# A later row turn, a re-ordered norm chain, four more taps on TensorE, and the last S5 weight loads behind the last state product

## Time and profile before

| what | us |
|---|---|
| median of 3 runs | 996.05 (995.78 to 996.17) |
| the profiled execution, its own time | 997.24 |
| its span, from first to last instruction | 995.4 |
| PE busy | 966.9 (97%) |
| DVE busy | 586.6 (59%) |
| ACT busy | 505.2 (51%) |
| POOL busy | 308.5 (31%) |
| mean granted TensorE clock | 0.993 of full speed |

### The profile page before, as it was taken

The page is one execution under the profiler, slowest core; times in us unless marked ns, Lnnn a source line. Parts: engine busy times, 40 slices in busy tenths (PEclk is TensorE's granted clock), DMA queues, the critical chain, the costliest instruction groups (busy, mean ns, idle before and its releaser), DMA issues.

```text
span 995.4 us, 14273 instructions
## 1 busy us (share of the span) xinstructions
PE 966.9 (97%) x5438; PEld 803.5 (81%) x5438; DVE 586.6 (59%) x643; ACT 505.2 (51%) x719; POOL 308.5 (31%) x331
## 2 busy tenths in 40 slices
PE   8999989999999989999999999999988999999997
PEld 6987768888878878888888888888978888888886
DVE  4899865555544455565674545446685764544534
ACT  5865455444443366446664444435465664444332
POOL 5770337888689505763010000000000020000000
PEclk9999899999999999999999999999999999999999
DMA  9832026676767727554446657567963455657541
GB/s 336 272 128 84 1 85 206 222 222 222 264 219 234 229 80 260 169 169 152 145 137 200 192 174 242 182 203 253 387 228 102 154 166 177 201 173 253 170 169 42
DMA packets 133827, 186.79 MB, mean 188 GB/s; under 512 B 5904, under 2 KB 104720, under 8 KB 133264
## 3 DMA queue, kind: packets, MB, share of 16 engines
q1 hardware_dynamic: 109632, 158.28, 49.1%
q10 hardware_dynamic: 24144, 27.81, 8.1%
HBM read 174.54 MB, written 15.73 MB: 191 GB/s over the span
## 4 chain that ended last, share of the span: by engine, by line
PE 85%; DVE 7%; DMA 3%; ACT 2%; issue 2%; POOL 1%; POOLq 0%; ACTq 0%; DVEq 0%
PE ps L508 24%; PE ps L480 15%; PE ps L482 14%; PE ps L481 14%; DVE cacc L2354 2%; PE ps L460 2%; PE ps L462 2%; PE ps L461 2%; DMA wraw<-in_w_in 2%; PE ps L1052 1%; PE ps L837 1%; PE ps L1071 1%; DMA O_dram<-ob 1%; PE ps L619 1%; PE ps L1157 1%
## 5 line engine op out<-in xcount | busy, mean ns | idle before, releaser
L420 DVE TENSOR_TENSOR wlo<-wraw,whi 128x2048 fp32r<-128x2048 f32 x127 | 303.1, 2388 | 298.2 <-ACT whi L414 298.2
L414 ACT ACTIVATE whi<-wraw 128x2048 fp32r<-128x2048 f32 x127 | 243.1, 1915 | 259.0 <-PE ps L482 159.5
L480 PE MATMUL ps<-whi,actH 128*128 128x512 f32 x640 | 257.8, 403 | 1.0 <-ACT qa L2107 0.6
L482 PE MATMUL ps<-whi,actL 128*128 128x512 f32 x640 | 250.2, 391 | 0.0
L481 PE MATMUL ps<-wlo,actH 128*128 128x512 f32 x640 | 249.4, 390 | 0.0
L480 PEld LDWEIGHTS ps<-whi,actH 128*128 128x128 f32 x640 | 120.3, 188 | 27.4 <-issue 2.3
L482 PEld LDWEIGHTS ps<-whi,actL 128*128 128x128 f32 x640 | 120.1, 188 | 26.1
L481 PEld LDWEIGHTS ps<-wlo,actH 128*128 128x128 f32 x640 | 120.5, 188 | 22.4
L754 POOL TENSOR_SCALAR ss<-ss 128x1 f32<-128x1 f32 x8 | 1.8, 220 | 439.6 <-ACT sg L724 439.6
L508 PE MATMUL ps<-whi,gH 128*128 128x512 f32 x248 | 77.8, 393 | 0.0
L508 PE MATMUL ps<-wlo,gH 128*128 128x512 f32 x248 | 76.8, 390 | 0.0
(11 more groups left out here) (452 smaller groups left out, 1574.2 us busy)
## 6 DMA issues: line engine op xcount, KB each, us to landing
wraw<-in_ffn_w_gate SPq DMA_DIRECT2D x44, 512.0 KB, 4.0
wraw<-in_ffn_w_up SPq DMA_DIRECT2D x44, 512.0 KB, 5.0
wraw<-in_ffn_w_down SPq DMA_DIRECT2D x18, 1024.0 KB, 4.9
wraw<-in_fox_w_in SPq DMA_DIRECT2D x16, 1024.0 KB, 5.5
wraw<-in_w_gate SPq DMA_DIRECT2D x22, 512.0 KB, 4.0
wraw<-in_w_up SPq DMA_DIRECT2D x22, 512.0 KB, 5.0
wraw<-in_w_in SPq DMA_DIRECT2D x9, 1024.0 KB, 11.4
wraw<-in_w_down SPq DMA_DIRECT2D x9, 1024.0 KB, 5.5
```

The costliest lines, as they stand in the source:

```text
L414: act.activation(self.high_of(n0), self.wraw[:, n0 % RAW, :], ACT.Copy).then_inc(self.hi_done, 1)
L420: dve.tensor_tensor(self.low_of(n0), self.wraw[:, n0 % RAW, :], self.high_of(n0).bitcast(F32), ALU.subtract).then_inc(self.lo_done, 1)
L480: pe.matmul(out, xh, wh, start=(ka == 0), stop=False)
L482: last = pe.matmul(out, xl, wh, start=False, stop=(ka == KT - 1))
```

## The change

It does the following. (a) `turn(1, 1)` moves from (row 1, unit n) to (row 0, unit n+1), in `f1` and `fp`. In `fp` the forget logits move back by two quarters, and their turn goes behind the whole of unit n+2; ACT splits n+2 ahead of the two squares, DVE ahead of the copy of the logits. (b) `SHARED` goes from 6 to 10: PE gets four more taps (one in the slot that had a single one, two after the scores of head 7, one after the values of head 5), ACT two more groups of diagonals, DVE loses its last four taps; one power table of ACT moves from head 6 to the later group. (c) ACT splits unit 9 after the first two q copies, and DVE splits it after four more taps. (d) In the norm chain, `centred` goes behind the first of DVE's four turned tiles, the copy of the sums goes ahead of the split of unit 12, and POOL's two sums wait for `ln_normed`. (e) `pool_prep` waits for the store only ahead of `ob`. (f) SP waits for `y_done` 4 ahead of the third gate unit.

```diff
@@ -37,7 +37,9 @@
...
 TAPG = 8
-SHARED = 6
+SHARED = 10
+TAIL_PAIRS = {21: 19, 23: 20}
+DIAGONALS_AT = {2: (0,), 3: (1, 2), 4: (3,), 5: (4,)}
 U_BANKS = (2, 3, 6, 7)
...
@@ -917,7 +919,7 @@
...
             self.mm_first_rows(pe, st, n, self.pair_banks(0), UNIT_BY_UNIT,
-                               {(0, 0, 2): lambda: turn(1, 0), (1, 0, 2): lambda: turn(1, 1)})
+                               {(0, 0, 2): lambda: turn(1, 0), (0, 1, 2): lambda: turn(1, 1)})
         else:
...
@@ -973,9 +975,8 @@
...
         s = b0 % 2
-        if b0 > 1:
+        if b0 > 1 and 0 in parts:
             pool.wait_ge(*self.past("prep_kmul", b - 1))
-            pool.wait_ge(*self.past(f"prep_stored{s}", 48 * half + 1))
         g = bass.ds(GB * b, GB) if step else slice(GB * b, GB * b + GB)
...
@@ -991,6 +992,8 @@
...
         if 1 in parts:
+            if b0 > 1:
+                pool.wait_ge(*self.past(f"prep_stored{s}", 48 * half + 1))
             times(o, self.F1, self.C1, T + 1).then_inc(done, 1)
...
@@ -1355,7 +1358,7 @@
...
     cmul(c, pool, (m.ZR[:], m.ZI[:]), (m.AR[:, :, 0:T], m.AI[:, :, 0:T]), z, (m.atmp[:], m.atmp2[:]),
-         lambda: m.pool_rstd(pool, "ln", AW, "ln_head_sums", 2))
+         lambda: (m.pool_rstd(pool, "ln", AW, "ln_head_sums", 2), pool.wait_ge(*m.past("ln_normed", 2))))
     pool.memset(m.zero1[:], 0.0).then_inc(m.sem("input_powers"), 1)
...
@@ -1481,6 +1484,9 @@
...
                         sp.wait_ge(*m.past("t_used", 1))
+                    if n == first["glu"] + 2:
+                        sp.wait_ge(*m.past("y_done", 4))
                     if n == first["o3"]:
...
@@ -1613,10 +1619,11 @@
...
                     pe.wait_ge(*m.past("v_out", 2))
-                if i >= 3 * (H1 - 1):
+                pair = i if i < 19 else TAIL_PAIRS.get(i)
+                if pair is None:
                     return
                 n = TAPS + SHARED
-                for s in range(2 * i, min(2 * i + 2, n)):
+                for s in range(2 * pair, min(2 * pair + 2, n)):
                     if s < TAPS:
...
@@ -1692,10 +1699,11 @@
...
             m.mm_first_rows(pe, "fp", n, (0, 1), UNIT_BY_UNIT,
-                            {(0, 0, 2): lambda: fp_turn(1, 0), (1, 0, 2): lambda: fp_turn(1, 1),
-                             (1, 1, 0): forget_logits, (1, 1, 2): forget_turned})
-            for h in range(2):
-                m.mm_half_k(pe, n + 2 + h, (4, 5), h)
+                            {(0, 0, 2): lambda: fp_turn(1, 0), (0, 1, 2): lambda: fp_turn(1, 1),
+                             (1, 1, 2): forget_logits})
+            m.mm_half_k(pe, n + 2, (4, 5), 0)
+            forget_turned()
+            m.mm_half_k(pe, n + 3, (4, 5), 1)
...
@@ -2012,8 +2020,9 @@
...
             act.activation(rinv[:, 0, 0:1], m.halfpi[:], ACT.Exp)
+            m.act_heads(act, "a1", m.qt, (0, 4), (4, 5), 0)
             m.split_high(act, 9)
-            m.act_heads(act, "a1", m.qt, (0, H1), (4, 5), 0)
+            m.act_heads(act, "a1", m.qt, (4, H1), (4, 5), 2)
             m.split_high(act, 10)
...
@@ -2032,11 +2041,11 @@
...
                     m.split_high(act, 11)
-                if 2 <= h < 5:
-                    shared_diagonals(h - 2)
+                for i in DIAGONALS_AT.get(h, ()):
+                    shared_diagonals(i)
                 if h == H1 - 1:
                     m.act_probs_turned(act, "a1", h, m.pt1, (6, 7))
-                if 3 <= h < 7:
+                if 3 <= h < 6:
                     act.wait_ge(*m.past("powers", 1))
...
@@ -2060,7 +2069,7 @@
...
             act.wait_ge(*m.past("input_powers", 1))
-            power_tables(4, 8)
+            power_tables(3, 8)
             m.act_row_turn(act, "f1", ROWS_LOW, 0, range(4), N2)
...
@@ -2085,9 +2094,9 @@
...
             forget_high()
+            m.split_high(act, first["fox"] + 2)
             for r in range(RT):
                 m.act_pre_square(act, "fp", "fp_x_ready", r, m.junkp)
-            m.split_high(act, first["fox"] + 2)
             m.split_high(act, first["fox"] + 3)
...
@@ -2405,13 +2414,14 @@
...
                 glu(j)
+            conv(4)
             m.split_low(dve, 9)
-            conv(10)
+            conv(6)
             m.split_low(dve, 10)
...
                 if h < 8:
-                    conv((6, 10, 11, 11, 11, 11, 2, 7)[h])
+                    conv((6, 10, 11, 11, 11, 11, 2, 3)[h])
                 if h == 2:
...
@@ -2434,13 +2444,12 @@
...
-            centred()
-            m.dve_turn(dve, "ao", (0, 1, 2), n=4)
+            m.dve_turn(dve, "ao", (0, 1, 2), n=4, between={1: centred})
             dve.wait_ge(*m.past("ln_sq", 1))
             dve.reduce_sum(m.csum[:], m.csq[:].rearrange("p j t -> p t j"), AX.X).then_inc(sem("ln_sq_sum"), 1)
-            m.split_low(dve, 12)
             dve.wait_ge(*m.past("ln_second", 1))
             dve.tensor_copy(m.ss[:, 0:2], ps[:, 3, 0:2]).then_inc(sem("ln_head_sums"), 1)
+            m.split_low(dve, 12)
...
@@ -2489,9 +2498,9 @@
...
             dve.tensor_tensor(m.wfL[:], m.wf[:], m.wfH[:].bitcast(F32), ALU.subtract).then_inc(sem("wf_split"), 1)
+            m.split_low(dve, n + 2)
             dve.wait_ge(*m.past("f_done", 1))
             dve.tensor_copy(m.fT[:], ps[0:H2, 3, 0:TOK]).then_inc(sem("f_out"), 1)
-            m.split_low(dve, n + 2)
...
```

## The result

The changed kernel takes 989.3 us (median of six runs, 988.04 to 991.64), the kernel before 996.11 in the same session (995.78 to 997.89). The ratio is 0.993, with an interval of 0.992 to 0.994: faster by 6.8 us. The profiled executions are 997.24 and 988.04, so they differ by more, 9.2 us; their spans are 995.4 and 986.2. The profiled execution of the changed kernel is its fastest. The control further down shows what the others lose.

A forecast was written before the change was run, and what follows sets the result against it. PE was taken to bound the kernel, busy 966.9 of 995.4 us; six parts (+0.8, -3.4, -1.7, -0.9, +0.4, -3.6) sum to -8.4, taken from the median 996.05 to give 987.7 us, range 984.8 to 992.0.

The forecast's parts named there:

- rival A: Attention's end: the clock falls anyway, so the gain there is only -1.1 us, total 990.0; chance 0.16.
- Part 1: Heads: q-copy wait goes (-1.07), but four taps delay DVE's split of unit 9 and PE waits; +0.8 us.
- Part 2: Attention end and norm chain: filled idle stretches keep the clock up, reordered norm chain cuts waits; -3.4 us.
- part 3: Row turn of `f1`: four more quarter rows done before the turn win 2.5 us, 0.8 goes back; -1.7 us.
- The give-back: In `f1`, unit 16's low half comes late for PE, so 0.8 us of the 2.5 won is lost again.
- Part 4: Store wait before block 10: POOL's `rtb` operations go ahead of it, so PE's wait for the block goes; -0.9 us.
- Part 5: `fp` row turn: gain largely offset by a new 2.9 us wait at unit n+3, clock taken as falling; +0.4 us.
- Part 6: S5 loads: holding weights back removes the 2.59 us issue stall and the clock loss behind it; -3.6 us.
- (B): S5: the stall isn't the weights' doing and stays, so the load edit wins 0; total 991.3 us; chance 0.11.
- (C): `f1`: POOL's tables pace PE, so the early gains of -4.3 us go back; total 992.0 us; chance 0.06.
- (E): Gate product: held-back loads start together and stall PE's next instruction page; slower by 2.8, 998.9 us; chance 0.05.
- (D): `fp`: the new wait doesn't arise because DVE splits n+3 earlier; -3.3 us more, total 984.4; chance 0.04.

The follow-up runs named there:

- the control: The changed kernel run once more, unaltered, beside the follow-up runs: 989.36 us, six runs from 988.11 to 991.8.
- the best order tried: Changed kernel with units 9, n+3, n+4 and n+5 split early, DVE taking n+4 ahead of the exponential wait, n+5 ahead of the keys' norm: 985.54 us.
- the first two moves: Changed kernel with n+3 split ahead of the turned logits: 990.2 us; with unit 9, n+3 and n+4 split early: 987.64 us against 987.67 with unit 9 alone.

## Why the prediction was right, and where it was not

The forecast was 987.7 us, within 984.8 to 992.0. The median is 989.3: inside the range and 1.6 us above the number, nearer to rival A's 990.0, though for another reason.

**Part 1** (+0.8) was +1.18. The mechanism is as written: four taps, then the split, and PE waits for it. Its term was mis-sized because DVE's split takes 2.83 us and not the 2.44 of the earlier trace rows; it began at 64.36, where I had 64.5. What the part left out is larger. It has an idle stretch of 2.2 us and no term for the clock behind it, which in the control is 1.7 us. I asked that question at parts 2 and 5 and not here. This is the step that failed: a wait priced by its length alone.

**Part 2** (-3.4) was -3.2: 2.5 us up to the output turn's last tile (116.45 before, 115.15 now, against 66.06 and 67.24), where I had 2.6, and 0.7 behind it, where I had 0.8. The clock holds through the sums, and the run with the same taps elsewhere shows that the filled stretches do it: 3.3 us when they are emptied; the order of the norm chain is 1.4 us by itself, where I had 1.3. The two together exceed 3.2; how they overlap was not tried.

**Parts 3 and 4** (-1.7 and -0.9) were -2.55 together. Undone, part 3 is 1.6 us of order, and 1.65 more of clock in that execution. The give-back is there, 0.77 us at unit 16, where I had 0.8. Part 4, undone, is not measurable (0.3 us in the medians, 0.5 in PE's wait): its 0.9 was the wait of one execution, taken for the price of an edit.

**Part 5** (+0.4) was -0.82 in the first profile, and 1.7 more, +0.9, where the clock fell. The new wait is 2.90 us, at 368.75, where I had 2.9 and, with the 4.55 us of the table taken off my 373.2, 368.6. Whether the clock falls behind it was a choice between -1.0 and +0.4, and the truth is both, in different executions. The cause and the wait I had right; the fall I had put at 1.4 us, from three windows of the earlier trace rows, and it measures 1.7. What it would win to take the wait away I had too simple: in three orders the wait moved on, or the norms came later.

**Part 6** (-3.6) was -3.6, and again -3.6 when made alone. Undone in the changed kernel it is 1.3 us in the profile and 0.9 in the medians, since the stall moved. So its worth depends on where the weights fall among PE's instructions, and there it is even less than -1.6, my end for "a second, shorter stall".

The sum of the parts in the first profile is -9.2 against -8.4. The medians moved by 6.8, which is 2.4 less: the profiled execution of the kernel before was 1.1 us above its median, that of the changed kernel 1.3 below. I had carried the sum over to the median as if executions differed only by a constant, and the two new waits, each with a clock that may fall behind it, make them differ by more. The runs at 989.4 and 991.7 lie about where one fall and two would put them; only executions of 988.0 and 991.8 were profiled, so for the one in the middle this is inferred. That the number came within 1.6 us is in part luck, since what the sum missed at the parts (-0.8) and what it missed in the clock have opposite signs.

Of the rivals none happened: the attention's clock held (A), the stall went (B), no table held PE (C), nothing stalled the gate units (E), and the wait of `fp` arose (D). D's price, 3.3 us, was not reached either: with n+3 split earlier PE waited 2.58 us for n+4, and the best order tried won 2.1 us in the medians, 1.7 of them clock.

## What to carry to other kernels

Price an idle stretch of PE twice, by its length and by the clock that may fall behind it, and do so at each place where the change makes one; of what this forecast left out in the heads, the second was the larger part. Where an order of splits makes PE wait, look for what would be late next before counting the gain: in `fp` the first two moves won nothing and the third only the clock, since each made something else late. Equal stages need not have equal causes: look whether PE waited at the end of the stage or was awaited. And a wait seen in one trace, or a stall that depends on where a transfer falls, is one sample: do the part alone and undo it in the changed kernel, since the two can differ (3.6 and 1.3 us).

## What the runs showed of the hardware

- One wait of 2.21 us, at 65.0 to 67.2 us in one execution and 0.7 us later in another of the same program, left the clock at 1.00 in the first and at 0.50 to 0.65 for nearly 4 us in the second. A stretch of 0.77 us in the attention's end, behind others, was enough to bring it down, where 0.28 us left it up. The length of the last wait does not decide it. The clock fell in five of eight executions behind the wait of 2.21 us (2.21 to 2.25) and in five of eight behind that of 2.90 us, and lost 1.7 us each time.
- PE's stall for "issue" ended 1.4 to 1.6 us after a packet of 16 KB on the queue of instructions was over, in both kernels that had such a stall, and the packets came some 3 to 5 us later than in the kernels without weights in the way (305 to 428 GB/s). The Trainium skill ("Runtime: NRT & Kernel Launch", Instruction fetch mechanics) has the fetch mostly hidden; in the products of block 3, behind full DMA engines, 1.10 and 2.59 us of PE's time were not, if these packets are what it waited for.
- DVE and POOL slow one another. DVE's split of unit 9 took 2.44, 2.83 and 2.40 us in three places, each time beside a POOL product, and 2.28 us at 366.41 with POOL idle. The POOL product beside the split of 2.83 us took 2.79 us, where it took 0.94 in the kernel with the split elsewhere. The two diagonals of the norm took 2.55 us before, beside POOL's sums, and take 0.48 us with the sums held back.
